# Two-block kernel on one core: the low parts of the second block's weight units are computed by GpSimd instead of VectorE, and GpSimd's pooling stands behind those of the first nine units

## What is computed

```
proj = einsum('bld,de->ble', h, w_in)          # q_r k_r v_r g_r u_p q_f k_f v_f f_logit
o_r  = silu(g_r) * head_group_norm(retention(rotary(q_r), rotary(k_r), v_r))
o_p  = multiscale_pool(u_p, pool_w, pool_scale)  # trailing means over 2, 4, 8, 16
o_f  = forgetting_attention(q_f, k_f, v_f, log_sigmoid(f_logit + b_f))
h = layer_norm(ALPHA * h + concat(o_r, o_p, o_f) @ w_out)
h = layer_norm(ALPHA * h + (silu(h @ w1) * (h @ w3)) @ w2)
```

## Time and profile before

| | |
|---|---|
| median of 3 runs | 3244.43 us (3243.34 to 3248.57) |
| the profiled execution, its own time | 3242.94 us |
| its span, first to last instruction | 3241.2 us |
| busy: PE, DVE, ACT, POOL | 2846.2 (88%), 952.0 (29%), 657.1 (20%), 72.3 (2%) us |
| mean granted clock of TensorE | 0.923 of full |
| first `raw` product of layer 0 and of layer 1 | 1664.53 and 2445.63 us from the start |

### The profile page before, as it was taken

One profiled execution on the slowest core, in us unless ns is written; L12 is line 12 of the kernel. 1 busy time (PEld: TensorE's weight loads), 2 busy tenths in 40 slices (PEclk: granted clock), 3 DMA queues, 4 the chain that ended last, 5 costly groups with the idle time before them and its releaser, 6 DMA issues.

```text
span 3241.2 us, 39408 instructions
## 1 busy us (share of the span) xinstructions
PE 2846.2 (88%) x17108; PEld 1997.0 (62%) x17108; DVE 952.0 (29%) x1570; ACT 657.1 (20%) x1124; POOL 72.3 (2%) x113
## 2 busy tenths in 40 slices
PE   2995967599999999999978978899998887899997
PEld 1442744433433433433457847899998675799996
DVE  2006563411111111111161243433234233433333
ACT  1001532110100010010032142322223223222222
POOL 0000000000000000000000200000000020000000
PEclk7996978699999999999989958999999986999999
DMA  9125101189999999999921101223241010232321
GB/s 313 55 84 213 35 1 54 48 344 410 410 409 410 409 409 410 410 409 410 396 58 53 46 14 53 66 80 97 83 106 52 28 59 1 57 90 83 105 73 51
DMA packets 319020, 558.59 MB, mean 172 GB/s; under 512 B 36818, under 2 KB 198996, under 8 KB 318509
## 3 DMA queue, kind: packets, MB, share of 16 engines
q1 hardware_dynamic: 307312, 548.48, 46.0%
q0 software_dynamic: 1552, 5.70, 0.5%
q10 hardware_dynamic: 10028, 2.53, 0.4%
HBM read 552.46 MB, written 4.23 MB: 172 GB/s over the span
## 4 chain that ended last, share of the span: by engine, by line
PE 76%; DMA 8%; DVE 8%; ACT 4%; issue 2%; ACTq 1%; SPq 0%; POOL 0%; DVEq 0%
PE vpsum L1819 20%; PE apsum L1819 11%; DMA ring<-w_down 8%; PE vpsum L1717 7%; PE vpsum L1734 7%; PE apsum L1703 4%; PE apsum L1828 3%; PE vpsum L1524 3%; PE vpsum L1761 2%; PE vpsum L1656 2%; PE apsum L1761 2%; PE apsum L1848 1%; PE apsum L1778 1%; PE vpsum L1585 1%; PE vpsum L1599 1%
## 5 line engine op out<-in xcount | busy, mean ns | idle before, releaser
L1717 PE MATMUL vpsum<-ring,arena 128*64 128x512 f32 x2048 | 449.4, 597 | 0.8 <-ACT arena L832 0.8
L1819 PE MATMUL apsum<-stream_r,wring_r 128*128 128x264 f32 x2880 | 371.7, 290 | 15.9 <-DVE stream_r L1277 15.9
L1819 PEld LDWEIGHTS apsum<-stream_r,wring_r 128*128 128x128 f32 x2880 | 364.2, 194 | 18.6 <-issue 15.8
L1819 PE MATMUL vpsum<-work_r,wring_r 128*128 128x264 f32 x2880 | 353.7, 285 | 3.3 <-DVE work_r L1400 3.3
L1819 PEld LDWEIGHTS vpsum<-work_r,wring_r 128*128 128x128 f32 x2880 | 353.0, 189 | 3.4 <-issue 3.4
L1305 DVE TENSOR_TENSOR wring_r<-wring,wring_r 128x2048 fp32r<-128x2048 f32 (+3 forms) x106 | 220.8, 2088 | 427.8 <-ACT wring_r L872 427.7
L1717 PEld LDWEIGHTS vpsum<-ring,arena 128*64 128x64 f32 x2048 | 144.9, 138 | 291.3 <-issue 291.3
L872 ACT ACTIVATE wring_r<-wring 128x2048 fp32r<-128x2048 f32 (+3 forms) x106 | 184.1, 1739 | 621.9 <-DMA wring<-w_ffn 600.9
L1819 PE MATMUL vpsum<-stream_r,wring_r 128*128 128x264 f32 x2400 | 298.2, 284 | 0.0
L1819 PEld LDWEIGHTS vpsum<-stream_r,wring_r 128*128 128x128 f32 x2400 | 293.8, 188 | 0.0
L1734 PE MATMUL vpsum<-ring,arena 128*64 128x512 f32 x1024 | 226.8, 595 | 38.5 <-DMA ring<-w_down 38.5
(11 more groups left out here) (392 smaller groups left out, 2655.9 us busy)
## 6 DMA issues: line engine op xcount, KB each, us to landing
ring<-w_gate SPq DMA_DIRECT2D x64, 2048.0 KB, 18.2
ring<-w_up SPq DMA_DIRECT2D x64, 2048.0 KB, 13.4
ring<-w_down SPq DMA_DIRECT2D x64, 2048.0 KB, 15.5
wring<-w_ffn SPq DMA_DIRECT2D x88, 512.0 KB, 4.7
ring<-w_ada SPq DMA_DIRECT2D x12, 2048.0 KB, 9.1
wring<-w_ffn SPq DMA_DIRECT2D x32, 704.0 KB, 4.5
ring<-w_in SPq DMA_DIRECT2D x5, 2048.0 KB, 16.8
wring<-w_in SPq DMA_DIRECT2D x10, 1024.0 KB, 5.5
```

The costliest lines, as they stand in the source:

```text
L1717: last = pe.matmul(bank[CAP * blk:CAP * blk + CAP, :], xin[:, 4 * r + c, :], w[:, c, 512 * blk:512 * blk + 512], start=r + c == 0, stop=r ...
L1819: last = pe.matmul(b[:, k, 0:HW], w_[:, c, col:col + P], halves(x[:, c, :])[:, k, :].bitcast(FR), start=c == 0 and i == 0, stop=c == chunk ...
```

## The change

GpSimd gets a function `weights_low` and all 106 low parts of both layers; DVE's function and all its calls are taken out. GpSimd's instructions are in this order in each layer: the wait for `par_done` and the four DMAs as before, the low parts of units 0 to 8, the pooling, a wait for its end, and then the low parts of units 9 to 52. ACT's high parts, SP's loads and PE's order stay as they are.

```diff
+        LU, LOW_FIRST = len(UNITS), K_U2
@@ gpsimd @@
+            def weights_low(l, ns):
+
+                for n in ns:
+                    pool.wait_ge(w_low, LU * l + n)
+                    pool.wait_ge(w_high, LU * l + n + 1)
+                    pool.tensor_tensor(unit_part(l, n, False).bitcast(FR), unit_part(l, n, False, wring), unit_part(l, n, True), ALU.subtract).then_inc(w_low, 1)
+                pool.wait_ge(w_low, LU * l + ns[-1] + 1)
+
...
                 VLl, ALl = VL.layer(l), AL.layer(l)
+                weights_low(l, range(LOW_FIRST))
                 pool.wait_ge(a_filled, ALl.count("ro3"))
...
                 mean(high, 1, sumB, last=True)
+                pool.wait_ge(pooled, l + 1)
+                weights_low(l, range(LOW_FIRST, LU))
@@ vector @@
-            def weights_low(l, n):
-                if l == LAYERS:
-                    return
-                dve.wait_ge(w_high, LU * l + n + 1)
-                dve.tensor_tensor(unit_part(l, n, False).bitcast(FR), unit_part(l, n, False, wring), unit_part(l, n, True), ALU.subtract).then_inc(w_low, 1)
...
-                    if h < 2:
-                        weights_low(l, 8 + h)
...
-                    if u in (3, 7, 11):
-                        weights_low(l, OP_U + 1 + u // 4)
...
-                for i in range(3):
-                    weights_low(l, FFN_U[0] + i)
```

More of the change, by code:

```diff
@@ L441, in program @@
             USED += [(VL, f"dn{g}", m) for m in range(KC)]
-        LU = len(UNITS)
+        LU, LOW_FIRST = len(UNITS), K_U2
         def unit_rows(n):
@@ L1311, in _ @@
             dve.tensor_copy(tri_r[:].bitcast(FR), tri).then_inc(mask_done, 1)
-            for n in range(3):
-                weights_low(0, n)
             norm(AE, "sum", "var", X0, colsB[:, 0:8], 0, colsB[:, 8:16])
@@ L1326, in _ @@
                 dve.wait_ge(q_zero, 2 * l + 2)
-                weights_low(l, 3)
                 def mix_low(c):
@@ L1346, in _ @@
                         dve.tensor_tensor(kr[:, j - 2, :], rtmp[:, 0, :], raw[:, j % 2, :], ALU.add).then_inc(rot_done, 1)
-                for n in range(4, 7):
-                    weights_low(l, n)
                 dve.wait_ge(a_freed, ALl.count("vc"))
@@ L1352, in _ @@
                 dve.tensor_tensor(f_in, vf[:, :, FH * FD:VF_W], bfb[:, l, :].rearrange("p (o h) -> p o h", o=1).broadcast_to([P, 5, FH]), ALU.add).then_inc(f_sum, 1)
-                weights_low(l, 7)
                 dve.wait_ge(f_ln, 3 * (l + 1))
@@ L1368, in _ @@
                             dve.tensor_tensor(retW[0:META, o + S:o + L2], b[0:META, S:L2], decay[0:META, h, 0:META], ALU.mult).then_inc(v_freed, 1)
-                    if h < 2:
-                        weights_low(l, 8 + h)
                 dve.tensor_copy(negc, flat(take("negc"))[0:FH, 0:L2]).then_inc(v_freed, 1)
-                weights_low(l, 10)
                 def by_group(x):
@@ L1385, in _ @@
                 dve.reduce_sum(gst[:, 1, :], squares20, AX_X).then_inc(o_var, 1)
-                weights_low(l, OP_U)
                 dve.wait_ge(o_rms, l + 1)
@@ L1441, in _ @@
                     for n in range(HALF_F):
-                        weights_low(l, FFN_U[g] + n + 3)
                         b = take(f"fu{g}", n)
@@ L1457, in _ @@
                             dve.tensor_tensor(x, x, b[:, :, 0:HW], ALU.add).then_inc(v_freed, 1)
-                        after = DOWN_U[g] + m + 3
-                        weights_low(l + after // LU, after % LU)
                 last = l == LAYERS - 1
```

## The result

The changed kernel took 3250.41 us (median of 20 runs, 3247.77 to 3256.46), the kernel before 3241.61 us beside it (20 runs, 3240.41 to 3255.29). The ratio is 1.0021, 95% interval 1.0013 to 1.0028: slower, by 4 to 9 us where 15.6 were forecast. The medians are 8.8 us apart. By the prediction's own band for "same" (3238 to 3251) it would just have counted as no change; the interval of the 20 runs is narrower than that band and clear of 1.

What follows compares the result with a forecast made beforehand. It took PE, three quarters of the chain of waits, as the bound. Losses of 25.8 less gains of 18.0 made 7.8 us a layer, 15.6 for both: median 3260.0 us, forecast 3253 to 3267, wider range 3249 to 3271.

Steps and rivals of the forecast that it cites:

- Start of the layer: First `raw` of each layer waits for GpSimd's low part of unit 0, clock included: 13.9 us lost a layer.
- Behind `vc`: DVE's L1355, with two SBUF inputs, waits for GpSimd's unit 7: 1.0 us lost a layer.
- `kf`: Its unit 9 stands behind the pooling: 8.7 us of waiting and 2.2 for the clock lost a layer.
- Heads 1 and 2: Steps from first score to `gr` fall to head 3's 4.05 us, `gr` regains 1.4: 10.8 us gained a layer.
- FOX: At steps 3, 7 and 11 DVE's low part goes but GpSimd blocks L1417: 4.4 us gained a layer.
- Rival 1: L1417 in FOX isn't blocked by GpSimd, so FOX gains 9.0 us a layer: 3250.8 us; chance 0.13.
- Norm behind `op`: DVE begins this norm when ACT's mean is there, without a low part ahead: 2.8 us gained a layer.
- Rival 3: Products with one PSUM input are blocked too, or GpSimd is at its upper end: 3270 us; chance 0.12.
- Rival 4: FOX gets the clock back, making the kernel faster; half of 31 us a layer would give 3229; chance 0.07.
- Rival 2: The clock isn't paid at the two stalls, layer start and `kf`: 2 x 4.4 us less, 3251; chance 0.08.

Runs made afterwards that it cites:

- e1: Changed kernel with GpSimd's low parts of units 0 to 2 ahead of its wait for `par_done` and the DMAs; 3240.76 us, 0.9991 to the kernel before.
- e7: Changed kernel, units 0 to 2 early (layer 0's on DVE), unit 9 ahead of the pooling, ACT's high parts of units 12 to 14 behind FOX; 3187.0 us.
- b3: Kernel before with only the low parts of units 9 and 10 moved to GpSimd, behind the pooling; 3252.1 us, 1.0034 to the kernel before.
- e2: Changed kernel with the low part of unit 9 also made ahead of the pooling; 3235.63 us, 0.997 to the kernel before.
- b1: Kernel before with only the low parts of units 8 and 9 moved to GpSimd, ahead of the pooling; 3218.76 us, 0.9917 to the kernel before.
- b2: Kernel before with only the low parts of units 12 to 14 moved to GpSimd, behind the pooling; 3233.53 us, 0.9975 to the kernel before.
- e4: Changed kernel with ACT's high parts of units 12 to 14 moved behind FOX's last step; 3228.41 us, 0.9948 to the kernel before.
- e8: e7 with the low part of unit 7 made by DVE, as before the change; 3186.49 us, 0.9829 to the kernel before.

## Why the prediction was right in direction and about twice too large

*Start of the layer* (13.9). Right in place and cause: 14.8, of which 0.5 is the low part's 4.6 us in place of 4.1. The half clock behind the stall came too: 0.50 in the changed kernel from 2470.9 to 2475.3. Of the 15.5 us by which layer 1's first `raw` starts later behind the norm, 2.1 are the four DMAs and 4.6 the subtraction; the larger part, 8.8, is the wait for `par_done` ahead of them, which comes when the norm is done. e1 and e7 take the stall away.

*Behind `vc`* (1.0). Right: 1.3 and 1.4.

*`kf`* (8.7 and 2.2). The wait was 8.8 and the clock 2.6 behind it (0.50 for 4.7 us, below), but 2.0 and 2.1 us came back up to FOX's first scores, which the prediction excluded: "so nothing of it is given back". b3 and e2 show the link: with the stall `key_bias` to FOX reads 2.8, without it 4.6. (e7's layer 1 reads 2.81 without it, so the stall is one way to it and not the only one.) Windows of the changed kernel behind the stall:

```profile
2644.80:2649.50 4.70, 4.65 (x21) 4.68 (x22) 0.00 (x0) 0.00 (x0) 2.35 (x1) 0.50 0.00 0
2649.50:2653.00 3.50, 3.50 (x28) 3.50 (x28) 0.00 (x0) 0.00 (x0) 0.00 (x0) 0.89 0.00 0
```

*Heads 1 and 2* (9.4 and 1.4). This is the step that failed: "Each falls to head 3's 4.05 us: 4.5 + 4.9. The `gr` behind them ... that is 1.4 back. Sum 10.8." The steps were right (9.3 in layer 1, of which 7.8 are the two waits of 3.73 and 4.09 us). The clock gain was put at 1.4 us, in the `gr` directly behind the gaps, and nothing for the last `ro` and `u`; the runs showed 3.0 us a layer more there. The clock had not stayed low up to that place: it was back at 1.00 for 20 us and fell to 0.50 once more in the last `ro`, with PE at work (windows above). The prediction had that row in hand (13.94 against 11.74) and read it as the price of a gap, which does not stand ahead of this `u`; it charged it to the new stalls and did not ask whether the change would move it. Heads, projections and `u` together gave 16.0 and 13.5 us where 10.8 were put. b1, with nothing but the heads freed, gives 15.1 and 10.8 over the same stretch, and b2's layer 1 loses the low clock in `u` without them. So that the heads' gaps decide over `u` is one reading; that any edit can shift where the clock falls is as well borne out.

*FOX* (4.4). The collision was right, the size only on average (2.5 and 5.3), and that in part by luck. Rival 1 falls: L1412 took 3.8 to 4.0 us in all three steps and both layers, where its shapes take 0.36 to 0.49 alone. The Trainium skill (SBUF — State Buffer, section "Who interferes with whom") has the rule that a DVE instruction in a two-port mode and GpSimd exclude each other for the whole instruction, and the trace agrees: 4.00 us beside the subtraction and 0.49 behind it. That L1412 runs in such a mode is inferred from these times. But the waits in FOX were exchanged rather than lost. In layer 1 PE's 12.2 us of waiting for the bias at L1409 became 2.7 (L1404 now), and 8.6 for L1412 came in. Windows over FOX before, layer 0 and 1 (those of the changed kernel are shown with e4):

```profile
1881.56:1966.70 85.14, 65.10 (x292) 38.83 (x293) 36.28 (x130) 39.91 (x128) 0.00 (x0) 0.63 0.00 1
2659.82:2746.66 86.84, 66.75 (x292) 39.65 (x293) 36.28 (x130) 39.92 (x128) 0.00 (x0) 0.62 0.00 1
```

PE's idle time fell by 1.8 and 2.0 us, not by 4.4; the other 0.7 and 3.3 us are the same matmuls in less time.

*Norm behind `op`* (2.8). Right: 2.8.

*Rivals 2, 3 and 4.* Rival 3 falls for products that read PSUM. Of head 1's products the last began within GpSimd's unit 8 and took 0.28 us as in the other heads, and the step from `rs` to `gr` took 4.13 us. DVE, then POOL, in layer 1, and then the 44 products of the feed-forward part with one input in PSUM, whose mean is the 704 ns of before although 30 of them began within a subtraction:

```profile
2568.07 0.62 DVE L1364 TENSOR_TENSOR body<-vpsum,body 128x256 f32<-128x256 f32 x2 [0.28 <-PE vpsum L1871]
```

```profile
2568.08 4.58 POOL L641 TENSOR_TENSOR wring_r<-wring,wring_r 128x2048 fp32r<-128x2048 f32 x1 [17.42 <-ACT wring_r L883]
```

```profile
L1435 DVE TENSOR_TENSOR body<-body,vpsum 128x528 f32<-128x528 f32 x44 | 31.0, 704 | 447.4 <-PE vpsum L1807 447.4
```

Rival 4's gain in FOX did not come (0.63 and 0.65 granted, 0.63 and 0.62 before), yet it had the right kind: the clock gave back more than was counted, mostly ahead of FOX. Rival 2, whose 3251 is the nearest to the time, came there for the wrong reason: the clock was paid at both stalls (0.50 each), but other places were not charged any more. None of the prediction's three signs of being wrong appeared (a low part far from 4.1 us, a wait in the feed-forward part, FOX above 0.7), so they could not have caught the step that failed.

In sum: the two stalls were priced well but for what comes back behind `kf`, and the steps that failed are the clock's share of the gains (1.4 us in the heads' `gr`, nothing behind it, nothing back from the `kf` stall) for which the runs show 3.0 us a layer in the last `ro` and `u` and 1.8 us at `key_bias`.

What stays open: by what the chip decides where it lowers the clock. The runs show that it repeats, that the same gaps can be followed by full or half clock in the same `u` (e1 13.6, the changed kernel 11.8 us), and that removing 1.3 us in e8 moved it to other places. I have no rule that would have given these from the trace of before.

## What to carry to other kernels

Work on an idle engine is free only where nobody waits for it: look at what stands ahead of it in that engine's list (here the wait for the norm's end, four DMAs of 2.1 us and the pooling of 20.4 us), and at which DVE instructions it blocks meanwhile. Where and when 7 of a layer's 53 low parts are made (units 0 to 2, 9 and 12 to 14) decided between 8 us slower and 56 us faster, and all three places showed as waits of PE in the changed trace. When a gap ahead of matmuls goes, the clock can change in places that have no gap of their own. List every stretch that the old trace shows at half clock, with what it costs against the same matmuls at full, and give the forecast a range for them; and compare whole stretches, since a gain of a us or two may be taken back behind it.

## What the runs showed of the hardware

- GpSimd subtracts 2048 f32 columns in 128 partitions in 4.61 us and 1408 in 3.25; DVE does the first in 2.3. On both its inputs were the weight unit and its high part.
- A one-input TENSOR_SCALAR from SBUF to SBUF on DVE (0.49 us) takes up to 4.04 us in the changed kernel (4.07 in b2) when it meets that GpSimd instruction, and six two-input instructions took 16.8 us beside three of them. Products with one input in PSUM were not held (704 ns on the mean of 44, before and after).
- The same `u` of 96 matmuls takes 11.9 or 13.7 us, and the 8 matmuls of `key_bias` 2.0 or 3.85, by the clock that they are granted; the choice was the same in two executions of one program and changed with edits tens of us ahead.
- The granted clock fell from 1.00 to 0.50 at 2590.0 us of the kernel before while PE was at work; over the 20 us ahead of it PE had been busy for 19.65.
